# Softmax sums of an attention stage: GpSimd adds four probability tiles instead of two, TensorE multiplies half as many sums by ones

## The reference

```python
s = einsum(qn, k_nope) + einsum(qr, k_rope)
p = softmax(s * scale, axis=-1)
o = einsum("bhqk,bkhd->bqhd", p, v)
```

## Time and profile before

| | |
|---|---|
| median of 3 runs | 1585.96 us (1586.0, 1584.27, 1585.96) |
| the profiled execution: its own time | 1584.54 us |
| the profiled execution: its span | 1582.7 us |
| attention stage within the span | about 600 to 820 us |
| PE busy, share of the span | 1497.3 us, 95% |
| DVE busy | 1003.1 us, 63% |
| ACT busy | 720.9 us, 46% |
| POOL busy | 406.3 us, 26% |

### The profile page before, as it was taken

How to read it: one execution, slowest core, us unless ns; L and a number is a source line. 1 busy time by engine, 2 the same in 40 slices (tenths; PEclk the granted TensorE clock), 3 DMA queues, 4 the chain that set the end, 5 groups by cost and what they waited for, 6 DMA issues and landing times.

```text
span 1582.7 us, 15796 instructions
## 1 busy us (share of the span) xinstructions
PE 1497.3 (95%) x5862; PEld 996.5 (63%) x5862; DVE 1003.1 (63%) x1014; ACT 720.9 (46%) x696; POOL 406.3 (26%) x209
## 2 busy tenths in 40 slices
PE   6999999999999999999999970999999999999997
PEld 3444487844344444555558860788888888888774
DVE  4533244442842564655635558699989989998886
ACT  3301000025422114355443341677777777777773
POOL 0031000000011003576673414023322223332204
PEclk9999999999999999999999985999999999999999
DMA  9311030115100000000123249699999999999994
GB/s 315 131 54 53 25 135 1 33 31 116 53 0 1 0 0 27 1 27 1 54 82 104 96 156 378 235 368 377 378 371 375 378 378 378 378 379 368 377 381 195
DMA packets 152886, 284.46 MB, mean 180 GB/s; under 512 B 25300, under 2 KB 35874, under 8 KB 152835
## 3 DMA queue, kind: packets, MB, share of 16 engines
q1 hardware_dynamic: 147219, 263.32, 46.8%
q0 software_dynamic: 4464, 16.25, 3.9%
q10 hardware_dynamic: 1152, 4.19, 0.6%
HBM read 259.10 MB, written 24.64 MB: 179 GB/s over the span
## 4 chain that ended last, share of the span: by engine, by line
PE 85%; DVE 6%; DMA 4%; ACT 2%; issue 2%; POOL 1%; SPq 0%; POOLq 0%; DVEq 0%; ACTq 0%
PE psum L1145 14%; PE psum L1605 9%; PE psum L1607 9%; PE psum L1606 9%; PE psum L1376 4%; PE psum L1238 3%; PE psum L1126 3%; DMA arena<-in_exp_w_down 3%; PE psum L1438 3%; PE psum L1346 3%; PE psum L1426 2%; PE psum L1091 2%; PE psum L1449 2%; PE psum L1427 2%; PE psum L1428 2%; PE psum L1254 2%
## 5 line engine op out<-in xcount | busy, mean ns | idle before, releaser
L2109 DVE TENSOR_TENSOR split_at<-arena,split_at 128x2048 fp32r<-128x2048 f32 x188 | 427.9, 2290 | 60.6 <-ACT split_at L1007 59.7
L1007 ACT ACTIVATE split_at<-arena 128x2048 fp32r<-128x2048 f32 x192 | 367.6, 1915 | 68.5 <-PE psum L1607 53.3
L1605 PE MATMUL psum<-split_at,split_at 128*128 128x512 f32 x768 | 305.9, 398 | 1.4 <-DVE split_at L2115 1.4
L1607 PE MATMUL psum<-split_at,split_at 128*128 128x512 f32 x768 | 300.2, 391 | 0.0
L1606 PE MATMUL psum<-split_at,split_at 128*128 128x512 f32 x768 | 299.5, 390 | 0.0
L1145 PE MATMUL psum<-arena 128*128 128x512 f32 x512 | 224.7, 594 | 1.4 <-DVE arena L1862 1.4
L1145 PEld LDWEIGHTS psum<-arena 128*128 128x128 f32 x512 | 96.1, 190 | 124.0 <-issue 123.9
L1607 PEld LDWEIGHTS psum<-split_at,split_at 128*128 128x128 f32 x768 | 144.5, 188 | 31.2
L1605 PEld LDWEIGHTS psum<-split_at,split_at 128*128 128x128 f32 x768 | 144.7, 188 | 29.7 <-DVE split_at L2115 1.8
L1606 PEld LDWEIGHTS psum<-split_at,split_at 128*128 128x128 f32 x768 | 144.9, 189 | 28.3
L1920 DVE TENSOR_REDUCE arena<-psum 128x1 f32<-128x1024 f32 x64 | 78.1, 1224 | 68.9 <-PE psum L1346 68.2
(11 more groups left out here) (302 smaller groups left out, 2219.3 us busy)
## 6 DMA issues: line engine op xcount, KB each, us to landing
arena<-in_exp_w_gate SPq DMA_DIRECT2D x64, 1024.0 KB, 14.4
arena<-in_exp_w_up SPq DMA_DIRECT2D x64, 1024.0 KB, 14.2
arena<-in_exp_w_down SPq DMA_DIRECT2D x64, 1024.0 KB, 14.4
arena<-in_w_in SPq DMA_DIRECT2D x9, 1024.0 KB, 8.4
arena<-in_x SPq DMA_DIRECT2D x8, 512.0 KB, 6.6
xhat_scratch<-arena SPq DMA_DIRECT2D x8, 512.0 KB, 10.0
arena<-in_w_out SPq DMA_DIRECT2D x8, 512.0 KB, 3.6
arena<-xhat_scratch SPq DMA_DIRECT2D x8, 512.0 KB, 4.8
```

The source lines that it names most:

```text
L1007: a(flat(wsplit[c % WS][0]), wraw[:, c], ACT.Copy).then_inc(s_whi, 1)
L1605: mm(bank(out_bank), src[0][:, k, :], whi[:, k % 4, :], start=(k == 0), stop=False)
L1607: ins = mm(bank(out_bank), src[1][:, k, :], whi[:, k % 4, :], start=False, stop=(k == KT - 1))
L2109: tt(flat(lo), wraw[:, c], flat(hi), ALU.subtract).then_inc(s_wlo, 1)
```

## The change

POOL forms two sums of four tiles in each head (`SETS = (4, 4)`) instead of four sums of two. `add_probs(n)` is called for each tile but the first of a set; the call for the second tile adds the first two into `p_pair[q % 2]`, each later one adds its tile to that buffer in place, after a wait for POOL's own add before it. That makes six additions a head for four. PE multiplies each finished sum by ones once (`sum_set`), at m = 3 and at m = 0 of the next head; the two products at m = 2 are gone. ACT's wait for the reading of tile n-4 counts the additions anew (`adds_done`). The waits of SP and DVE on `s_sum` name the same points with new counts.

```diff
+        SETS = (4, 4)
+        N_SET = len(SETS)
+        def set_of(kb):
+            return next(m for m in range(N_SET) if kb < sum(SETS[:m + 1]))
+        def adds_done(n):
+            h, kb = divmod(n, TT)
+            opened = set_of(kb)
+            return (TT - N_SET) * h + kb - opened + (kb == sum(SETS[:opened]))
...
-            sp.wait_ge(s_sum, 4 * NH - 4)
+            sp.wait_ge(s_sum, N_SET * NH - N_SET)
...
-            sp.wait_ge(s_sum, 4 * NH - 1)
+            sp.wait_ge(s_sum, N_SET * NH - 1)
             sp.dma_start(xres[:, 0, :], xh_tok[:, 0, :]).then_inc(s_xh[0], 16)
...
-            def add_pair(q):
-                pool.wait_ge(s_exp, 2 * q + 2)
-                if q >= 2:
+            def add_probs(n):
+                h, kb = divmod(n, TT)
+                m = set_of(kb)
+                q, opening = N_SET * h + m, kb == sum(SETS[:m]) + 1
+                pool.wait_ge(s_exp, n + 1)
+                if opening and q >= 2:
                     pool.wait_ge(s_sum, q - 1)
-                b = 2 * (q % 2)
-                pool.tensor_tensor(p_pair[q % 2], p_at[:, b, :], p_at[:, b + 1, :], ALU.add).then_inc(s_pa, 1)
+                if not opening:
+                    pool.wait_ge(s_pa, adds_done(n) - 1)
+                total = p_pair[q % 2]
+                pool.tensor_tensor(total, p_at[:, (n - 1) % 4, :] if opening else total, p_at[:, n % 4, :], ALU.add).then_inc(s_pa, 1)
...
                 for n in range(TT * h, TT * h + TT):
-                    if n % 2 == 0 and n >= 4:
-                        add_pair(n // 2)
+                    if n % TT not in OPENS:
+                        add_probs(n)
+                    if n == 3:
+                        head_low(1, 0)
+                        head_low(1, 1)
...
-                    act.wait_ge(s_pa, n // 2 - 1)
+                    act.wait_ge(s_pa, adds_done(n - 4))
...
-            def sum_pair(q):
+            def sum_set(q):
-                h, m = divmod(q, 4)
-                pe.wait_ge(s_pa, q + 1)
+                h, m = divmod(q, N_SET)
+                pe.wait_ge(s_pa, (TT - N_SET) * h + sum(SETS[:m + 1]) - m - 1)
...
                         if m == 0 and h:
-                            sum_pair(4 * h - 1)
+                            sum_set(N_SET * h - 1)
...
                     if m == 2:
-                        sum_pair(4 * h)
-                        sum_pair(4 * h + 1)
                         for qt in slots.get((2, 2), ()):
                             rough_next(h + 1, qt)
                     if m == 3:
-                        sum_pair(4 * h + 2)
+                        sum_set(N_SET * h + 0)
...
-            sum_pair(4 * NH - 1)
+            sum_set(N_SET * NH - 1)
```

More of the change, by code:

```diff
@@ L489, in _ @@
             sp.wait_ge(s_gb, 32)
-            sp.wait_ge(s_sum, 4 * NH - 1)
+            sp.wait_ge(s_sum, N_SET * NH - 1)
             sp.dma_start(xres[:, 0, :], xh_tok[:, 0, :]).then_inc(s_xh[0], 16)
-            sp.wait_ge(s_sum, 4 * NH)
+            sp.wait_ge(s_sum, N_SET * NH)
             for dst, src in ((gmix, A["ln_mix_g"][0]), (bmix, A["ln_mix_b"][0])):
@@ L574, in head_low @@
                     pool.tensor_tensor(lo[0:DV, :], k_at[h // 4][:, h % 4, :], hi[0:DV, :], ALU.subtract).then_inc(s_qkp, 1)
-            def add_pair(q):
-                pool.wait_ge(s_exp, 2 * q + 2)
-                if q >= 2:
-                    pool.wait_ge(s_sum, q - 1)
-                b = 2 * (q % 2)
-                pool.tensor_tensor(p_pair[q % 2], p_at[:, b, :], p_at[:, b + 1, :], ALU.add).then_inc(s_pa, 1)
-            for h in range(NH):
[L585 to L589, removed]
-                for n in range(TT * h, TT * h + TT):
-                    if n % 2 == 0 and n >= 4:
-                        add_pair(n // 2)
+            def add_probs(n):
[4 more added lines that the diff above has]
+                if opening and q >= 2:
+                    pool.wait_ge(s_sum, q - 1)
+                if not opening:
+                    pool.wait_ge(s_pa, adds_done(n) - 1)
+                total = p_pair[q % 2]
+                pool.tensor_tensor(total, p_at[:, (n - 1) % 4, :] if opening else total, p_at[:, n % 4, :], ALU.add).then_inc(s_pa, 1)
+            OPENS = [sum(SETS[:m]) for m in range(N_SET)]
+            for h in range(NH):
+                for n in range(TT * h, TT * h + TT):
+                    if n % TT not in OPENS:
[3 more added lines that the diff above has]
+                        head_low(1, 1)
                     if h and h + 1 < NH and n % TT in (1, 3):
@@ L1449, in sum_pair @@
                     ins = mm(bank(7, 1, DV * j, DV * j + DV), ones[:, 0:DV], p_pair[q % 2][:, HALF * j:HALF * j + HALF],
-                             start=(m == 0), stop=(m == 3))
+                             start=(m == 0), stop=(m == N_SET - 1))
                 ins.then_inc(s_sum, 1)
@@ L1960, in sums_inverse @@
                 if c == 0:
-                    v.wait_ge(s_sum, 4 * h + 4)
+                    v.wait_ge(s_sum, N_SET * (h + 1))
                 v.reciprocal(bank(7)[:, cols], bank(7)[:, cols]).then_inc(s_oi, 1)
```

## The result

| | before | changed |
|---|---|---|
| median | 1585.68 us (4 runs) | 1575.60 us (4 runs, 1575.14 to 1576.51) |
| ratio, 95% interval | | 0.9943 (0.9931 to 0.9955) |
| profiled execution: time, span | 1584.54, 1582.7 us | 1575.77, 1574.0 us |
| forecast | | 1574.7 us (1571.3 to 1578.0) |

The change makes the kernel 10.1 us faster by these medians. The forecast of 1574.7 was 0.9 us too low.

A forecast was written before the change was run, and what follows sets the result against it. PE was taken to set the pace. Gains of 0.47 (head 0) + 10.26 (heads 1 to 6) - 0.29 (head 7) = 10.44 us, from the four executions' mean of 1585.19, gave 1574.7 us, range 1571.3 to 1578.0.

The forecast's parts named there:

- 1.71 us a head by the removal: Heads 1 to 6: dropping the two products with ones at m = 2 saves 1.71 us each, 10.26 us together.
- The 0.47 us to spare before the transposition: Heads 1 to 6: the rough score's maximum is ready at 762.77, 0.47 us before the transposition at 763.24.
- rival 2: Heads 1 to 6: a later row maximum loses 0 to 1 us a head, giving 1577 to 1580 us; 10 in 100.
- Head 0, 0.47 us: Between head 0's two rough scores: the second must wait for DVE's maximum, so only 0.47 of 1.71 us is gained.
- POOL's ten instructions: Heads 2 to 6: POOL has ten instructions instead of eight, stays idle 2 us a head and does not fall behind.
- Rival 3: Heavy heads: POOL becomes the bound, kernel slower from a step of 2.76 us; 1595 us at 2.9 us; 3 in 100.
- Head 7: Last head: PE waits about 2.5 us for POOL, last sum 0.77 us late, part comes back; net -0.29 us.
- the forecast by starts: End of head 7: POOL's instructions timed from start to start put the last sum at 818.87.
- the one by spans: End of head 7: POOL's instructions timed by their durations, 2.38 us each, put the last sum at 818.7.
- let part of it come back: After head 7's last sum: PE's 0.48 us idle before the output projection makes up part of the 0.77 us lost.
- rival 4: Whole kernel: the change does nothing measurable because its products lie beside other work; 1 in 100.
- rival 1: Last head costs nothing: the whole 13.7 us shows, for heads 0 and 7 too, giving 1571.5 us; 6 in 100.

The follow-up runs named there:

- Head 7 in pairs: The changed kernel with heads 0 to 6 in sets of four and head 7 in pairs as before the change: 1573.91 us.
- DVE's help: The changed kernel with the low parts of output weights 6 and 7 made by DVE instead of POOL in head 7: 1571.66 us.
- PE's filler: The changed kernel with ten products, whose results nobody reads, put before the last product with ones: 1574.41 us.
- the repeat: The changed kernel run once more without any edit: 1576.22 us, 8.5 us below the kernel before in its own comparison.
- one set of eight: The changed kernel with one sum of all eight tiles a head, seven additions and one product with ones: 1580.32 us.
- the kernel with one set: The changed kernel with one sum of eight tiles a head and all output weights' low parts made by DVE: 1570.20 us.

## Why the prediction was right, point by point

- **1.71 us a head by the removal** was right: copies of heads 1 to 6 are 25.81 to 25.84 us apart. They gained 0.35 us more than six times 1.71, 0.2 of it in head 2, which took 27.79 us before where the others took 27.54 to 27.57. The 0.47 us to spare before the transposition held; rival 2 did not come. (By its own 0 to 1 us a head that rival spans 1574.7 to 1580.7, not 1577 to 1580.)
- **Head 0, 0.47 us**: measured 0.48. That DVE's maximum is what is late was shown by moving other work between the rough scores.
- **POOL's ten instructions**: 25.83 us a head and 1.8 to 2.0 us idle, as worked out. How near the limit this is, one more instruction a head showed (4.1 us slower). Rival 3 needed a step of 2.76 us, or eleven steps.
- **Head 7**: the last sum was forecast 0.77 us late and came 0.88 late, with a pause of 2.65 us (2.5). The chained steps of 2.49 to 2.52 us, for 2.48, are the 0.1. From POOL's first addition in head 7 to the last sum it was 808.63 - 789.30 = 19.33 us; the forecast by starts has 19.21, the one by spans 19.04, so the starts were the better reading here.
- **The term that failed** is the one that let part of it come back, "After the last sum PE did 819.06 to 824.64 of other products": the sum shifted this stretch with its old length. At the lower clock it was 7.19 us instead of 5.58, so that in all 0.97 us was lost where 0.48 had been counted as regained. Where the clock stayed up after the same pause, the sum held (7.45 for 7.55). The prediction looked at the clock only in the router stage and held that the change does not touch it. Head 7 in pairs, DVE's help and PE's filler each removed the pause, and each had 5.57 to 5.59 us there.
- **The total was in part luck.** The stage gained 9.24 us for a sum of 10.44, so the forecast was 1.2 too high where it can be checked. The medians' 10.1 lies nearer to the 10.44 than the 8.5 of the repeat, and the difference is spread of the runs.
- **Doing nothing (rival 4)** and **the last head costing nothing (rival 1)** are both out: the kernel is 8.5 to 10.1 us faster, and PE waits 2.65 us in head 7, where pairs are 2.3 us better.

## What to carry to other kernels

Work taken off a full engine is worth its time only where something is queued right behind it: look at what each removed piece had hidden (head 0) and who must deliver last (head 7). When additions move to an engine with room on average, count its instructions in the period of one head and again behind the last arrival. The last round may want another division than the others.

## What the runs showed of the hardware

- **A pause can cost the clock behind it.** PE idle for 2.60 to 2.65 us before the last sum was followed by the level of 1.2 GHz in two of three profiled executions, and idle for 3.61 to 7.41 us in all four; with no pause, one of 0.28 us, or the pause filled with products, in none of five (the kernel before among them). It costs 1.6 us there in the changed kernel. The length alone does not decide: with one set of eight a wait of 1.43 us in head 6 was followed by the low level, one of 1.24 us a head earlier (736.07) was not, nor were the two of 1.32 us in head 0 of the changed kernel, nor one of 2.63 us. The Trainium skill, TensorE: Matmul & The Clock Gate, The HAM clock gate, calls the low level the default that activity lifts; these executions agree in that the level fell behind pauses and rose again under work (1.00 from 814 us on in the changed kernel).
- **DVE and POOL wait for each other when DVE reads two operands from SBUF.** 1.2 us alone, up to 3.4 beside a POOL addition, whose own time rose from 2.38 to 3.3 in turn. DVE's row maxima, which read PSUM, took 1.21 to 1.23 us, all 64. The Trainium skill, SBUF — State Buffer, Who interferes with whom, states that a VectorE instruction with two inputs in SBUF contends with a GpSimd instruction that reads SBUF, and that the contention is an exclusive lock. The trace agrees: the longest subtraction, 3.42 us, stays just under 1.2 us alone plus one addition of 2.38. POOL lost about 1.7 us by it at the end of the kernel with one set.
- A GpSimd addition in place that waits for the one before it costs 2.49 to 2.52 us from start to start, 0.15 to 0.18 more than the 2.34 of an independent one.
